# Recurrent (Mamba-2) stage of a hybrid decoder step: one weight stream, then one scan over all groups and chunks

## What is computed

```python
xbc = silu(causal_conv(h @ W_xbc))            # 3072 columns: x 2048, B 512, C 512; 4 taps
dt, A = softplus(dtr + bias), -exp(a_log)
Acs = cumsum(dt * A) within a chunk           # per head
m = (C B^T) * exp(Acs_l - Acs_s) * dt_s       # s <= l
y_diag = m x
state' = state * exp(Acs_end) + B^T (x * exp(Acs_end - Acs) * dt)
y_off = (C state) * exp(Acs)
y = (y_diag + y_off + d_skip * x) * silu(z)   # z = h @ W_z, 2048 columns
y = y * rsqrt(mean over a group of y^2 + eps) * norm_g
```

## Time and profile before

| | |
|---|---|
| median of 3 runs | 3225.16 us (3214.72 to 3228.82) |
| profiled execution: time, span | 3218.5 us, 3216.7 us |
| busy over the span: PE, DVE, ACT, POOL | 91%, 50%, 22%, 22% |
| mean granted TensorE clock | 0.941 of full |
| recurrent stage, first z unit on PE to first DMA issue of merge | 1085.72 to 1956.06 us: 870.3 us |
| of it group 0's z phase, to its first chunk | 96.7 us |
| group 3's chunk phase | 90 us, PE busy 62.0 us |

### The profile page before, as it was taken

The page is one execution under the profiler, slowest core; times in us unless marked ns, Lnnn a source line. Parts: engine busy times, 40 slices in busy tenths (PEclk is TensorE's granted clock), DMA queues, the critical chain, the costliest instruction groups (busy, mean ns, idle before and its releaser), DMA issues. The chain is left out here.

```text
span 3216.7 us, 39531 instructions
## 1 busy us (share of the span) xinstructions
PE 2922.9 (91%) x15831; PEld 2373.2 (74%) x15831; DVE 1607.0 (50%) x2872; ACT 716.8 (22%) x1459; POOL 720.1 (22%) x439
## 2 busy tenths in 40 slices
PE   7999999989976879999999965999879999999997
PEld 5887566657864656775766844999869898898986
DVE  3323699435542446636456463254563444445455
ACT  3122211046741114324334252000030000000001
POOL 0000600032200122222132243232232232232320
PEclk9999999979985789999999987999989999999999
DMA  6110254300012220121210105322201111111111
GB/s 203 56 40 27 84 157 150 119 30 1 2 59 86 70 80 27 44 79 43 67 56 30 50 17 184 110 88 92 100 27 53 40 53 40 40 53 40 40 40 53
DMA packets 220322, 211.57 MB, mean 66 GB/s; under 512 B 15273, under 2 KB 201505, under 8 KB 219954
## 3 DMA queue, kind: packets, MB, share of 16 engines
q1 hardware_dynamic: 194412, 158.14, 16.1%
q10 hardware_dynamic: 20944, 34.86, 3.1%
q0 software_dynamic: 4784, 16.05, 1.3%
HBM read 165.32 MB, written 43.83 MB: 65 GB/s over the span
## 5 line engine op out<-in xcount | busy, mean ns | idle before, releaser
L2064 PE MATMUL ps<-h_lo,w_hi 128*128 128x344 f32 x1504 | 483.2, 321 | 38.6 <-DVE h_lo L2172 31.8
L2065 PE MATMUL ps<-h_hi,w_hi 128*128 128x344 f32 x1504 | 481.9, 320 | 0.0
L2066 PE MATMUL ps<-h_hi,w_lo 128*128 128x344 f32 x1504 | 481.8, 320 | 0.0
L2064 PEld LDWEIGHTS ps<-h_lo,w_hi 128*128 128x128 f32 x1504 | 284.5, 189 | 40.3 <-issue 35.5
L2046 POOL CAST w_hi<-w_raw 128x2048 fp32r<-128x2048 f32 (+1 forms) x50 | 97.2, 1944 | 836.0 <-PE ps L2066 801.3
L2065 PEld LDWEIGHTS ps<-h_hi,w_hi 128*128 128x128 f32 x1504 | 284.1, 189 | 0.2
L2066 PEld LDWEIGHTS ps<-h_hi,w_lo 128*128 128x128 f32 x1504 | 284.3, 189 | 0.0
L1526 PE MATMUL ps<-hT,ring 128*128 128x344 f32 x864 | 263.3, 460 | 0.0
L1605 PE MATMUL ps<-ring,hT 128*128 128x256 f32 x1024 | 237.8, 394 | 7.8 <-PEq L1176 6.8
L465 PE MATMUL ps<-ring,hT 128*128 128x256 f32 (+3 forms) x1152 | 238.0, 369 | 5.9 <-PEq L119 5.9
L2048 POOL TENSOR_TENSOR w_lo<-w_raw,w_hi 128x2048 fp32r<-128x2048 f32 (+1 forms) x50 | 233.7, 4675 | 4.0
(11 more groups left out here) (398 smaller groups left out, 5018.8 us busy)
## 6 DMA issues: line engine op xcount, KB each, us to landing
ring<-in_w_ada SPq DMA_DIRECT2D x24, 1024.0 KB, 7.5
ring<-in_w_in SPq DMA_DIRECT2D x23, 1024.0 KB, 5.2
w_raw<-in_w_ffn_in SPq DMA_DIRECT2D x44, 512.0 KB, 5.0
ring<-in_w_in SPq DMA_DIRECT2D x24, 512.0 KB, 8.3
w_raw<-in_w_ffn_out SPq DMA_DIRECT2D x10, 1024.0 KB, 5.0
s_sig<-sig ACTq DMA_DIRECT2D x16, 516.0 KB, 6.8
x<-s_sig ACTq DMA_DIRECT2D x16, 516.0 KB, 3.3
stt<-in_state_ssm SPq DMA_DIRECT2D x32, 256.0 KB, 3.6
```

Of the source, the lines that this page charges most:

```text
L2064: nc.tensor.matmul(out, ah, bl, start=(i == 0), stop=False)
L2065: nc.tensor.matmul(out, ah, bh, start=False, stop=False)
L2066: mm = nc.tensor.matmul(out, al, bh, start=False, stop=(i == len(terms) - 1))
```

## The change

`ssm` is split in two blocks with a boundary between them.

`stream` does all that needs weights: four z blocks of group 0, then for groups 1 to 3 six x/B/C blocks and four z blocks, 34 blocks of 128 features. Each block is three units of 8 matmuls with 344 columns, 102 units in one row on PE with four PSUM banks; z now has features on partitions, and the sample columns come with it. ACT applies Silu to z and stores each z block to DRAM (s_z); the convolved and activated x, B and C blocks go to DRAM as well (s_post). The sample recurrence stands at fixed unit numbers. At its start PE forms the running sums of the decays as rows per head (8 small matmuls); DVE splits them in two fp32r parts, and POOL puts them in a small table (segw) and in DRAM.

`scan` then runs over n = 4 c + g, all four groups of a chunk before the next chunk, 32 passes. It reads the chunk of post and z back from DRAM (SP, four buffers), and stores y (three buffers). The states of the four groups stay in SBUF. y has features on partitions and is summed in PSUM: the skip term as a product with a diagonal matrix, eight diagonal products with 64 stationary columns that write the two halves of the partitions in turn, and the carried part as a product with the identity. The segment sums come from fp32r matmuls with 18 rows and a mask. The root is exp(-0.5 ln(mean + eps)) on ACT; the sum over the group comes from a matmul with ones.

```diff
+        blocks = [("z", 0, j) for j in range(4)]
+        for g in range(1, GROUPS):
+            blocks += [("x", g, f) for f in range(FBS)] + [("z", g, j) for j in range(4)]
+        NU = TC * len(blocks)
+        z_end = [12 + 30 * g for g in range(GROUPS)]
+        raw_at = [11 if g == 0 else z_end[g] - 10 for g in range(GROUPS)]
+        spread_at = [[raw_at[g] + 3, raw_at[g] + 7] for g in range(GROUPS)]
+        sum_at = [raw_at[g] + 12 for g in range(GROUPS)]
...
+            for u in range(NU + 4):
+                if u < NU:
+                    unit(u)
+                for g in range(GROUPS):
+                    if u == raw_at[g]:
+                        raw_rows(g)
...
+def scan(K, S):
+    N = TT * GROUPS
+    NIN, NOUT = SEG_BUFS, 3
...
+            for n in range(N):
+                if n >= NIN:
+                    sp.wait_ge(skip_ps, n - NIN + 1)
+                sp.dma_start(post[:, n % NIN], ...)
+                if n >= NIN:
+                    sp.wait_ge(ygated, n - NIN + 1)
+                sp.dma_start(z[:, n % NIN], ...)
+                if n >= NIN + 2:
+                    store(n - NIN - 2)
...
+            def front(n):
...
+                if n >= 3:
+                    pe.wait_ge(ylog, n - 2)
+                tr(ps[:, CB_B, BT], x[:, 4], K.ident[:])
+                mm(ps[:, CB_B, CB], x[:, 4], x[:, 5], start=True, stop=True).then_inc(cb_ps, 1)
...
+                for half in range(2):
+                    mm(ps[:, SEG + half, :], S.segw[:, g, c, :], S.segm[:, n % NIN, 4 * P * half:4 * P * half + 4 * P],
+                       start=True, stop=False)
+                    t = mm(ps[:, SEG + half, :], later[:], ident4[:].rearrange("p h l -> p (h l)"), start=False, stop=True)
...
+            def diagonal(n):
+                for r in range(GH):
+                    lanes = slice(HD * (r % 2), HD * (r % 2) + HD)
+                    t = mm(ps[lanes, Y_T + n % 2, P * (r // 2):P * (r // 2) + P], xdt[:, n % 2, HD * r:HD * r + HD],
+                           m[:, n % 2, r, :], start=False, stop=(c == 0 and r >= GH - 2))
...
+            front(0)
+            for n in range(N + 1):
+                if GROUPS <= n < N:
+                    carried(n)
+                if n < N:
+                    skip(n)
+                if n + 1 < N:
+                    front(n + 1)
+                if n < N:
+                    diagonal(n)
+                    new_state(n)
+                if n:
+                    sum_squares(n - 1)
+                if GROUPS <= n < N:
+                    add_carried(n)
...
+            def root(n):
+                act.wait_ge(ysum_ps, n + 1)
+                a.activation(logs[:, n % 2], ps[:, CB_B, SQ], ACT.Ln, bias=eps[:, 0:1], scale=1.0 / GW).then_inc(ylog, 1)
+                act.wait_ge(ylog, n + 1)
...
+                a.activation(spreads[:, n % 2], logs[:, n % 2], ACT.Exp, scale=-0.5).then_inc(yinv, 1)
...
+            for n in range(N + 1):
+                if n >= 2:
+                    root(n - 2)
+                if n:
+                    square(n - 1)
+                if n + 1 < N:
+                    keep_b(n + 1)
+                    decay(n + 1)
+                    weigh(n + 1)
...
+            for n in range(N + 2):
+                if 1 <= n <= N:
+                    gate(n - 1)
+                if GROUPS <= n < N:
+                    scale_carried(n)
+                if n + 1 < N:
+                    prepare(n + 1)
+                if n >= 2:
+                    divide(n - 2)
+                if n < N:
+                    advance(n)
+                if n + 1 < N:
+                    mask(n + 1)
```

More of the change, by code:

```diff
@@ L1366, in ssm, with nth @@
             "sample_ssm_step", "ysq_done", "ysq_summed", "yroot_arg", "yroot_done"))
[L1367 to L1375, removed]
         old_out = K.store_sem("old_conv_rows_stored")
         block = ctx.enter_context(nc.Block())
[L1381 to L1390, removed]
+        blocks = [("z", 0, j) for j in range(4)]
[6 more added lines that the diff above has]
+        sum_at = [raw_at[g] + 12 for g in range(GROUPS)]
+        last_unit = {(b[1], b[2]): TC * i + TC - 1 for i, b in enumerate(blocks) if b[0] == "x"}
+        def nth(kind, i):
+            return sum(1 for b in blocks[:i] if b[0] == kind)
         def states(g, q, name):
@@ L1397, in _, with load_slab @@
         def _(sp):
[L1398 to L1403, removed]
+            def load_slab(n):
+                for place, src in K.slabs[n]:
+                    sp.dma_start(place(K.ring[:, n % RING, :]), src).then_inc(K.landed[n % RING], 16)
             def load_conv_rows(g):
@@ L1422, in exchange_states, with conv_rows @@
                     load_states(h + 1)
[L1424 to L1432, removed]
+            def conv_rows(g):
                 sp.wait_ge(rows_done, 2 * (g + 1))
@@ L1516, in _, with unit @@
             tr, mm = nc.tensor.transpose, nc.tensor.matmul
-            def unit(g, j):
-                f, c, u = j // TC, j % TC, FBS * TC * (g - 1) + j
-                if j % (2 * TC) == 0:
-                    pe.wait_ge(*ring_landed(K, slab(g, f // 2)))
-                if u >= 2:
-                    pe.wait_ge(pre_done, u - 1)
-                w = slab_of(K, slab(g, f // 2))
+            def unit(u):
+                i, c = u // TC, u % TC
+                n = first + i // 2
+                if u % (2 * TC) == 0:
+                    pe.wait_ge(*ring_landed(K, n))
+                if u >= 4:
+                    kind, before = blocks[(u - 4) // TC][0], (u - 4) // TC
+                    pe.wait_ge(*((z_done if kind == "z" else pre_done), TC * nth(kind, before) + (u - 4) % TC + 1))
+                w = slab_of(K, n)
@@ new lines, in keep_x @@
+            def keep_x(u):
+                i, c = u // TC, u % TC
+                q = FBS + nth("x", i)
+                act.wait_ge(gemm, u + 1)
+                if c == 0:
+                    act.wait_ge(conv_done, q - NPRE + 1)
+                    act.wait_ge(tails, q - NPRE + 1)
+                a.copy(pre[:, q % NPRE, CONV - 1 + CW * c:CONV - 1 + CW * c + CW], ps[:, u % 4, 0:CW]).then_inc(pre_done, 1)
+            first_silu = [3, 4, 6, 8, 9, 11]
+            for u in range(NU + 6):
+                if u < NU:
+                    (keep_z if blocks[u // TC][0] == "z" else keep_x)(u)
+                if u in first_silu:
+                    silu(first_silu.index(u))
+                for (g, f), end in last_unit.items():
+                    if u == end + 3:
+                        silu(FBS * g + f)
+                for g in range(GROUPS):
+                    if u == raw_at[g]:
@@ L1954, in scale @@
[L1954 to L1969 removed]
+            dve.wait_ge(acs_ps, 1)
@@ new lines, in _ @@
+            both = ps[0:HEADS, 4:6, :].rearrange("h a n -> h (a n)")
+            v.tensor_copy(acs[:, 0, :], both).then_inc(acs_done, 1)
+            dve.wait_ge(acs_done, 1)
+            v.tensor_tensor(acs[:, 1, :], both, acs[:, 0, :], ALU.subtract).then_inc(acs_done, 1)
+            for f in range(FBS):
+                convolve(0, f)
+            sample_conv(0)
+            sample_states(0, 0)
+            convolve(1, 0)
+            sample_states(0, 1)
+            convolve(1, 1)
+            sample_gate(0)
```

810 lines of the change are left out of this document (420 added, 390 removed).

## The result

The changed kernel takes 3127.84 us in the median of four runs (3122.04 to 3132.16). The kernel before, run on the same chip beside it, takes 3226.01 (3214.72 to 3228.82). The ratio is 0.9701, with a 95% interval of 0.9672 to 0.973: 3% faster, 98 us. The forecast was 3120, with a range of 3088 to 3185. (Its own steps, 3118.5 for the profiled execution and 6.7 for the median above it, add up to 3125; it took 3120.)

The account below looks back on a forecast made before the run. PE bound group 0's chunk phase, the chunk chain group 3's. New stage: 3 + 475.5 + 23 + 8.5 + 8 + 239 + 13.5 = 770.5 against 870.3 us, so 3118.5 profiled, 3120 taken; range 3088 to 3185.

Parts of the forecast that it names:

- Stream: Weight units on PE: 102 at 4.63 us, 3 for low-clock start, 3 for running sums, 23 for sample work; no stalls.
- Tail and boundary: Group 3's sample chain beyond the last units, 8.5 us; then new block's entry and first chunk's landing, 8 (bounds 4 and 11).
- The scan: 32 passes at ACT's pace of 7.15 us, 228.8, plus 7 to fill the line and 3 for low clock: 239.
- four fp32r products of 512 columns at 0.23: 0.92: PE's segment products in each scan pass, priced by attention's row; the old form was 1.7 us.
- filling the line and the low clock: Start of the scan: 7 us for the first pass to fill the line, 3 for PE starting at low clock.
- ACT's list: ACT's work in one scan pass: sum 7.0, with gaps 7.15 us, longest of the engines by little; xw products 1.74.
- The diagonal products: Eight per scan pass on PE: 0.98 us taken from attention's row, 1.73 if halves did not overlap.
- End: From the last matmuls to merge's first issue: 11.5 us before, 13.5 forecast with four final states instead of one.
- A drain behind each table load: Rival in the scan on ACT: 1.38 us stall behind each of 64 loads, 88 us, total 3207; chance 0.04 including equal losses elsewhere.
- The store of y: Rival: y's store holds DVE's gate; 7.1 us landing gives 8.8 a pass, 3173; chance 0.20 including another ring.
- The clock: Rival: PE stays at 1.2 GHz in the scan, pass 13.2 us, up to 3315; chance 0.07 including an unseen stall.
- The scan runs on PE's pace: Rival: shorter ACT passes let PE's 6.7 pace, 3106; or non-overlapping halves give 7.45, 3130; within the forecast range's 0.64.

Follow-up runs that it names:

- runs on order, 128 and 64 rows: Each against the changed kernel: segment products ordered 18, 18, 128, 128 (ratio 0.9671); their 18 rows zero-filled to 128 (0.9648); zero-filled to 64 (0.9709).
- with full rows: Changed kernel with the segment products' 18 rows filled with zeros to 128, order unchanged; 3101.73 us, ratio 0.9648.
- Grouping: Changed kernel with the eight diagonal products going four times to the lower half, then four times to the upper, instead of alternating; 3139.37 us, ratio 0.9759.
- keeping PE busy ahead: Changed kernel with twenty unread products of 128 columns ahead of the scan's first transpose; 3128.54 us, ratio 0.9701.
- the last experiment: Changed kernel plus rows zero-filled to 128, xw products on POOL, final states in two banks, squares folded twice on POOL for one PE product; 3090.2 us, ratio 0.959.

## Why the prediction came out as it did

The time was right within 8 us, by a sum of which one term named the wrong engine and several others were off in both directions.

- **Stream.** Forecast 3 for the sums and 475.5 + 23 for units and sample work, 501.5 in all; measured 3.15 and 493.5 (from 1086.26 to the last unit's end, 1579.8), 4.8 less. The unit was right within 0.03 us: L1499 is busy 474.9 us, 4.66 a unit. That leaves 18.6 for the sample work on PE, instead of 23. The 3 us of low-clock start did not occur: the running sums stand ahead and the clock is 1.00 from the first unit on. PE has no idle time between 1086.26 and 1579.8, so DVE's sample work is hidden as argued.
- **Tail and boundary.** Forecast 8.5 + 8; measured 8.85 for both, 7.7 us less. The tail, a wait of 2.50 for the squares of the samples and their sum of 1.06, is 3.6: it was over-sized by 4.9, since little of group 3's sample chain stuck out behind the last unit. The boundary, the wait of 5.29 for the first chunk, is 2.7 under the 8 taken and inside its bounds of 4 and 11.
- **The scan.** Forecast 239; measured 252.3, 13 more. The step that failed is "four fp32r products of 512 columns at 0.23: 0.92". They took 1.72. The row was for products that all use 128 rows; I took its price for a sequence that alternates 18 and 128. The runs on order, 128 and 64 rows settle why: 0.2 us for each change, none without it, and as much from 64 rows. The Trainium skill, "TensorEngine Tiling (Array Packing)", section "Key Properties", says that changing the tiling mode (not just the tile) drains the TensorE. If weights of 18 or 64 rows run in another mode than weights of 128, each alternation costs by that rule; the trace agrees, with 0.2 us a change. The four products are 0.8 us dearer and the step into the first of them another 0.15 (from L1881 to L1889 0.43 us, with full rows 0.28), so PE's pass was 7.66, above its own upper end of 7.45 and above ACT's 7.0, and PE paced. 32 x (7.66 - 7.15) is 16 us. What is left of the 252.3 us, 7.2, stands against the 10 forecast for filling the line and the low clock, and that it is so near is luck: 2.1 of it are waits and work behind the last carried product, and the first four passes have no carried part (0.86 and 0.89 us each), which hides 7 us. Filling and low clock together cost about 12.
- **ACT's list** was near as a sum (7.15 forecast, 6.92 back to back with full rows), wrong in its parts: the xw products took 2.0 instead of 1.74, and several steps overlap the next by about 0.1 where I added 0.02.
- **The diagonal products**, the largest unknown of PE's list, took 1.02 for eight, against 0.98 taken and 1.73 feared. Grouping shows that the alternation is what makes them cheap.
- **End.** Forecast 13.5, measured 16.7. PE and ACT take turns over one bank (waits of 1.79, 0.77 and 0.77): four final states are no longer hidden in units.
- **Rivals.** A drain behind each table load: no, 0.01 us. The store of y: DVE's gate waited for no DMA in the steady scan. The clock: 1.00 there; only the first 35 us ran at 0.73, and keeping PE busy ahead gave 3 us and cost as much. "The scan runs on PE's pace" was the case that occurred, but not for a reason it named: I had PE pace only if ACT's passes came out shorter or the halves did not overlap, and it was the segment products.

In sum: stream 4.8 less, tail and boundary 7.7 less, scan 13.3 more, end 3.2 more: 4 us over, 774.5 against 770.5. That it came so close is partly luck, since errors of 12.5 and 16.5 us have opposite signs. The rest of the kernel took 3125.48 - 774.5 = 2351.0 where before it took 3218.5 - 870.3 = 2348.2, 3 us that I don't explain; executions of one kernel differ by more (3214.72 to 3228.82 before). That the samples' columns in the units save what their own products cost, some 32 us by the rows, was read and not tested by a run of its own.

## What to carry to other kernels

Price an instruction by a row with the same neighbours, not only with the same shape: a matmul's price includes whether its weights can be loaded under the one before. Where products with few rows stand between full ones, put equals together, or fill the small ones with zeros to full height; that took 0.7 us from a pass of 7.7 and cost two instructions on POOL ahead of it. And when two engines are within a few per cent of each other, an error in either list swaps the pacer: state what both lists would give, since relief for the wrong one (here the log and the table loads) buys nothing.

## What was not expected of the hardware

- A change in the number of rows that the weights use costs about 0.2 us (0.43 against 0.23 for 512 columns of fp32r), for 18 to 128 and for 64 to 128 alike, and the weight load then starts with its own product's record, not under the product before. Between full rows and weights of 64 columns the step seems smaller (last segment product to first diagonal one 0.32 us instead of 0.23, with full rows).
- A fp32 product of 64 stationary columns takes 0.13 us in alternating halves and 0.19 in one half, against 0.22 for 128 columns.
- Twenty products of 128 columns after an idle stretch took 7.4 us at a granted clock of 0.59, where four of the same size take 0.89 in the scan at full clock (L1925 above), so 4.4 for twenty. Here they delayed what followed by as much as the clock they brought back was worth, or by more.
- DVE's four divides take 1.61 us in the kernel after and 2.12 in the last experiment, where POOL's second fold and its xw product run beside them; that POOL slows them was not tested by itself. DVE had slack for it.
